# Two attention branches of a decoder's prompt stage: another order of four steps inside each beat of the pair loop

## What is computed

```
s = einsum('bqgjd,bgqnld->bgjqnl', q, k) * scale
p = masked_softmax(s, mask)
o = einsum('bgjqnl,bgqnld->bqgjd', p, v)
o = g0 * o_cmp + g1 * o_sel + g2 * o_win        # sigmoid gates
```

## Time and profile before

| what | us |
|---|---|
| median of 3 runs | 1639.38 |
| lowest, highest | 1632.87, 1643.29 |
| the profiled execution, whole time | 1641.88 |
| its span, first to last instruction | 1640.1 |
| of it the pair loop (first S to last F) | 567.9 to 806.7 |
| busy over the whole span: PE, DVE, ACT | 1461.0, 871.5, 383.5 |

### The profile page before, as it was taken

One profiled execution on the slowest core, in us unless ns is written; L12 is line 12 of the kernel. 1 busy time (PEld: TensorE's weight loads), 2 busy tenths in 40 slices (PEclk: granted clock), 3 DMA queues, 4 the chain that ended last, 5 costly groups with the idle time before them and its releaser, 6 DMA issues. The chain is left out here.

```text
span 1640.1 us, 27038 instructions
## 1 busy us (share of the span) xinstructions
PE 1461.0 (89%) x11343; PEld 1342.2 (82%) x11343; DVE 871.5 (53%) x1590; ACT 383.5 (23%) x891; POOL 82.5 (5%) x76
## 2 busy tenths in 40 slices
PE   6999899889968797989766689999989999999998
PEld 5778789789958586868543389899988999999998
DVE  3555256848633556564433355545746746465563
ACT  3543023222232344454221231000003101000000
POOL 1000001100011111111100000000000000000000
PEclk8999999999967697979678789999999999999999
DMA  9232035151321000010258442333240332323321
GB/s 351 72 116 97 13 95 184 56 201 57 119 53 53 0 1 1 2 52 2 100 190 312 175 124 79 107 99 95 91 156 26 104 104 78 103 80 99 93 88 53
DMA packets 115649, 159.03 MB, mean 97 GB/s; under 512 B 6040, under 2 KB 106840, under 8 KB 112779
## 3 DMA queue, kind: packets, MB, share of 16 engines
q1 hardware_dynamic: 111886, 122.76, 23.4%
q0 software_dynamic: 2304, 33.56, 5.1%
q10 hardware_dynamic: 1348, 1.12, 0.2%
HBM read 145.04 MB, written 16.66 MB: 99 GB/s over the span
## 5 line engine op out<-in xcount | busy, mean ns | idle before, releaser
L330 PE MATMUL ps<-uH,wh 128*128 128x260 f32 x576 | 165.9, 288 | 8.7 <-DVE wt L301 8.7
L330 PE MATMUL ps<-hH,wh 128*128 128x260 f32 x512 | 144.9, 283 | 2.6 <-DVE hT L301 2.6
L330 PE MATMUL ps<-mergedH,wh 128*128 128x260 f32 x512 | 145.7, 285 | 0.0
L330 PE MATMUL ps<-mergedT,wh 128*128 128x260 f32 x512 | 144.8, 283 | 0.0
L330 PE MATMUL ps<-hT,wh 128*128 128x260 f32 x512 | 144.8, 283 | 0.0
L330 PE MATMUL ps<-mergedH,wl 128*128 128x260 f32 x512 | 144.5, 282 | 0.0
L330 PE MATMUL ps<-hH,wl 128*128 128x260 f32 x512 | 144.5, 282 | 0.0
L457 PE MATMUL ps<-XT,w 128*128 128x256 f32 (+1 forms) x512 | 125.5, 386 | 6.3 <-DVE XT L520 6.0
L330 PEld LDWEIGHTS ps<-uH,wh 128*128 128x128 f32 x576 | 109.9, 191 | 13.6 <-DVE wt L301 8.9
L330 PE MATMUL ps<-uL,wh 128*128 128x260 f32 x384 | 109.1, 284 | 0.0
L330 PE MATMUL ps<-uH,tw 128*128 128x260 f32 x384 | 109.0, 284 | 0.0
(11 more groups left out here) (525 smaller groups left out, 3470.8 us busy)
## 6 DMA issues: line engine op xcount, KB each, us to landing
wt<-in_w_ff SPq DMA_DIRECT2D x32, 1024.0 KB, 5.4
wt<-in_w_in SPq DMA_DIRECT2D x15, 1024.0 KB, 5.7
tw<-in_w_in SPq DMA_DIRECT2D x12, 1024.0 KB, 5.3
ring<-in_cache_mem_kv SPq DMA_DIRECT2D x4, 2048.0 KB, 11.2
w<-in_cmp_w SPq DMA_DIRECT2D x8, 512.0 KB, 7.7
ring<-in_cache_win_kv SPq DMA_DIRECT2D x2, 2048.0 KB, 9.8
out_s_win<-in_cache_win_kv SPq DMA_DIRECT2D x1, 4088.0 KB
scratch_uhigh<-uH SPq DMA_DIRECT2D x1, 2080.0 KB
```

The source lines that it names most:

```text
L330: ins = pe.matmul(out, lhsT(i, c), rhs(j, c), start=(first and c == 0 and k == 0), stop=(last and c == chunks - 1 and k == 2))
```

## The change

In each beat, V(u-2) moves ahead of both turns of unit u-1 on PE. E(u) moves ahead of both copies of unit u-1 on ACT. F(u-2) moves on DVE from the end of the beat to right behind B(u) or close to it. The keys of the steps are spread anew, so the DeltaNet steps that fall in between fall in other gaps. No instruction is added or taken away, and the waits are the same.

```diff
--- before (pair_pe)
                     if u < NU:
                         scores(u)
                     yield beat(u, 0.3)
+                    if u >= 2:
+                        values(u - 2)
+                    yield beat(u, 0.55)
                     if 1 <= u <= NU:
                         turn(u - 1, 0)
-                    yield beat(u, 0.5)
-                    if u >= 2:
-                        values(u - 2)
-                    yield beat(u, 0.6)
+                    yield beat(u, 0.75)
                     if 1 <= u <= NU and rounds_of(u - 1) == 2:
                         turn(u - 1, 1)
--- before (pair_act)
                     yield beat(u, 0.35)
+                    if u < NU:
+                        exp(u)
+                    yield beat(u, 0.6)
                     if 1 <= u <= NU:
                         keep(u - 1, 0)
-                    yield beat(u, 0.55)
-                    if u < NU:
-                        exp(u)
-                    yield beat(u, 0.65)
+                    yield beat(u, 0.8)
                     if 1 <= u <= NU and rounds_of(u - 1) == 2:
                         keep(u - 1, 1)
--- before (pair_dve)
                     if u < NU:
                         biggest(u)
-                    yield beat(u, 0.8)
+                    yield beat(u, 0.45)
                     if u >= 2:
                         finish(u - 2)
                         dve.wait_ge(o_done, u - 1)
```

## The result

The changed kernel takes 1654.08 us (median of 4 runs, 1652.68 to 1659.21), the kernel before, measured beside it, 1638.47 (1632.87 to 1643.29). The ratio is 1.0093 with a 95% interval of 1.0059 to 1.0128: slower by a little under one per cent. The profiled execution of the changed kernel took 1659.21, the longest of its runs. The code ahead of the pair loop is the same, and yet the first S starts at 574.52 instead of 567.94. Over the thirteen profiled executions of this study that start lay between 564.0 and 574.5, so two spans can't be compared to better than some 10 us. The loop itself is compared more closely: from the first S to the last F it took 238.8 us before and takes 249.4 now, 10.6 more. Behind the loop the two executions differ by 0.1 us. So the 17.3 us between the two profiled executions are 6.6 ahead of the loop, which the change doesn't touch, and 10.6 in it.

The account below looks back on a forecast made before the run. PE was taken as the bound, busy 205.75 of 238.00 us in the pair loop. Terms 7.2 + 5.4 + 3.0 - 3.5 - 3.8 + 5.1 = 13.4 us on the median 1639.4 gave 1653, range 1635 to 1670.

Parts of the forecast that it names:

- beats 20 to 25: Three-tile beats 21 to 25: second turn, or E in beat 23, comes later; 7.2 us lost.
- beats 28 to 38: Four-tile beats 30 to 35: mostly later second turns, beat 32 gaining 0.5; 5.4 us lost in all.
- tail: After the last E: K(38, 0), T(38, 1), K(38, 1) and an unhidden copy join the path; 3.0 us lost.
- beats 0 to 19: One-round beats: gains from F(9), E(13) and 0.3 elsewhere; together 3.5 us gained.
- beats 26, 27: S(27) starts 0.8 us earlier and the beat after runs at full clock, 3.0; 3.8 us gained.
- clock, apart: New PE gaps bring three more low-clock stretches, each costing up to 1.75 us; 5.1 us lost.
- The second turn behind E: Two-round beats: T(u-1, 1) waits for S, B, E, K; 4.3 us after S with three tiles, 5.1 with four.
- The second rival: DeltaNet products fill the time before T(u-1, 1), leaving the tail's loss against gains: -4 us, about 1635; chance 0.17.
- F(9) and E(13): Beats 12 and 13: F(9) ahead of the second chunk's end gains 1.9 us; E(13) ahead of chunk steps, 1.3.
- The 0.8 of E(26): Beat 26: E(26) goes ahead of the third chunk's root and table load, so S(27) starts 0.8 us earlier.
- The zero for the other load: Beat 27: the table load moves to E(27), behind K(25, 1) and beside V(25), and costs nothing.
- the first rival: Two-round beats: PE's clock stays low, about 0.7 from 664 to 696; 10 us more, about 1663; chance 0.22.

Follow-up runs that it names:

- mixed kernel: The changed kernel with PE and ACT back in the old order in beats where unit u-1 has two rounds; 1636.09 us, ratio 0.9975.
- DVE-only kernel: The kernel before, with only F(u-2) moved to 0.45 of the beat on DVE, PE and ACT as before; 1638.64 us, ratio 0.9984.
- ACT-only kernel: The kernel before, with only ACT's new order, E(u) ahead of both copies of unit u-1; 1653.65 us, ratio 1.0090.
- tail_old: The changed kernel with the old order on PE and ACT for u of 39 and more; 1653.75 us, ratio 1.0091.
- beat 26, put together by hand: The kernel before, with new order in beats 0 to 14 and beat 26's PE, ACT and DVE steps reordered; 1625.76 us, ratio 0.9903.
- the mixed kernel with the early F: The mixed kernel with F(u-2) at 0.37 of the beat on DVE instead of 0.45; 1639.72 us, ratio 1.0006.

## Why the prediction was right, and where it was not

It said 1653 (1635 to 1670), and the median is 1654.08. Step by step the agreement is less even:

```
term                            predicted   measured
beats 20 to 25                      +7.2      +6.92
beats 28 to 38                      +5.4      +6.69
tail                                +3.0      +2.91
beats 0 to 19                       -3.5      -6.00
beats 26, 27                        -3.8      +0.09
clock, apart                        +5.1      in the rows above
sum                                +13.4     +10.61
```

- **The second turn behind E.** Right in place, mechanism and price. The five beats from 21 on lost 1.12, 1.91, 0.85, 1.74 and 1.34 us, for 1.35, 2.0, 0.7, 1.8 and 1.4 in the prediction. That ACT's order alone costs as much in the beats 20 to 25 (38.08), and that the mixed kernel loses all but 0.8 of it, shows the cause. What the prediction did not see is that V's new place has a price of its own there: with E back in its old place 4.7 of the 6.9 us remain, by the copy right behind the first turn. The second rival, that DeltaNet products fill the time, is refuted by the 14 waits. With four tiles the agreement of the sum, 6.69 for 5.4, hides misses. In the beats 31 and 35 I said 1.7 and 1.4, and it was 1.47 and 1.31. Beat 30 lost 2.19 for 1.7. Beat 32 gained nothing where I had 0.5, and in beat 34 I had 1.1 and it was 0.6 faster. Beat 37 I held for covered; its second turn waits 0.77 us and it costs 0.95. The five beats of the term come to 4.35; the rest is that 0.95, a loss of 2.3 by the clock in beat 28, and small gains elsewhere.
- **The tail.** 2.91 for 3.0, shown by the kernel that puts it back.
- **F(9) and E(13).** 1.81 for 1.9 and 1.40 for 1.3. F's part is shown by the DVE-only kernel, and beat 12 takes 4.9 us in all nine executions that have both new orders there. E's part is shown by the ACT-only kernel, where S(14) starts without its wait of 1.56. Its size is partly luck: with the wait gone, beat 13 took from 5.97 to 8.17 us over those nine executions, at clocks from 0.71 to 0.50, against 8.72 before.
- **Beats 26 and 27**, the step that failed: "with the gap gone, the beat after at full clock, 3.0". The 0.8 of E(26) came, with 0.67, and the gap ahead of S(27) went: S(27) starts right behind the second turn and takes 1.03 us. But two other gaps took its place, and the sum had no term for either. V(25) waits 1.65 us for F(24), which is still behind the chunk's end on DVE, and from there to the end of beat 28 PE ran mostly at half clock. And the second turn of beat 26 waits 1.44 us for a copy that stands behind the chunk's root and its table load:

```profile
707.38 0.60 ACT L1401 ACTIVATE g_sq<-ps 128x512 f32<-128x512 f32 x1 [0.52 <-PE ps L1363]
708.00 1.28 ACT L1403 ACT_TABLE_LOAD   x1
709.29 0.20 ACT L1403 ACTIVATE g_so<-g_so 128x4 f32<-128x4 f32 x1
709.40 0.46 ACT L1704 COPY XT<-ps 128x384 f32<-128x384 f32 x1
```

  The zero for the other load was right. It runs from 711.06 to 712.34, ahead of E(27), which waits for its B until 713.71; and the root above starts 0.01 us behind its load, as in the earlier trace rows. An earlier F made these beats 4.5 us shorter. The lesson is in the account: the stall that goes was priced and the one that is late next was not.
- **The clock.** "I take three" half-clock stretches more, 5.1 us. None of it came. With five gaps of 0.57 to 1.73 us in the beats 21 to 25 the clock stayed at 1.00, and so it did in the window from 756 to 800, in which the second turn of beat 34 waits longest:

```profile
770.59 0.63 PE L1631 MATMUL ps<-consts,Pb 128*128 128x128 f32 x4 [2.82 <-ACT XT L1704]
...
756.00:800.00 44.00, 39.33 (x310) 34.11 (x310) 20.91 (x44) 18.41 (x43) 5.07 (x4) 1.00 0.00 1
```

  Over the loop the mean clock rose from 0.87 to 0.90. So the first rival, a clock that stays low, did not happen, and half-clock time fell: by this share from some 62 us (0.26 of 239) to 50. That is where 2.4 us of beat 16 came from, while beat 28 lost 2.3 by it. The fall is not the change's doing for certain: `tail_old`, with the same order up to beat 38, has 0.88, so some 60 us.

That the number came out so close is in part luck. Two errors, the 5.1 of the clock and the 3.9 of the beats 26 and 27, had opposite signs. The early gain was 2.5 larger than I said in this execution, and 0.7 smaller in five others with that order. The sum for the loop, 13.4, was 2.8 above the loop's 10.6. The medians differ by 15.6, within an interval of 9.7 to 21 us, which holds both. No trace shows where the median has its other 5 us; the stages ahead of the loop scatter by 10, and the early beats of one order by 3.

## What to carry to other kernels

In a pipeline written out by hand, list for each in-order engine what a moved step now stands behind, and follow a buffer with one copy (here the bank of the turns) through that list: a step that looked free because it ran beside another becomes the longest chain of the beat once its release stands behind an operation of the same beat. Keep two orders where the units differ (one round, two rounds), and look at places where a second program's long chain ends: beat 26, put together by hand, is 2.35 us shorter at nearly the same clock, nearly as much as the whole new order is worth in the beats 0 to 19 of most executions (2.8). When a stall is removed, price the next one before its gain is booked.

## What the runs showed of the hardware that I had not expected

**The same gap does not always bring TensorE's clock down.** Three kernels have the same order in the beats 26 and 27 and the same gap ahead of S(27). Here are S(27) and a window behind it for the kernel before, the DVE-only kernel and the mixed kernel, in this order:

```profile
703.54 2.07 PE L1620 MATMUL ps<-kmT,qmT 128*128 128x256 f32 x4 [2.23 <-ACT Pb L1695]
...
703.00:713.00 10.00, 9.46 (x41) 9.00 (x42) 3.94 (x15) 2.94 (x10) 2.08 (x2) 0.50 0.00 0
```

```profile
704.87 1.92 PE L1620 MATMUL ps<-kmT,qmT 128*128 128x256 f32 x4 [2.23 <-ACT Pb L1695]
...
705.00:711.00 6.00, 6.00 (x37) 5.54 (x38) 2.15 (x9) 2.07 (x7) 1.43 (x2) 0.72 0.00 0
```

```profile
702.61 1.13 PE L1620 MATMUL ps<-kmT,qmT 128*128 128x256 f32 x4 [2.24 <-ACT Pb L1701]
...
702.00:708.00 6.00, 5.39 (x44) 5.07 (x46) 3.78 (x14) 3.12 (x10) 2.16 (x2) 1.00 0.00 0
```

Ten microseconds at 0.50, a part of six, and none: beat 27 took 9.83, 6.84 and 5.17 us. In these two beats the steps stand in the same order on PE, ACT and DVE in all three traces. So one execution may be 4.7 us off from another there by nothing in the order of these beats. In this kernel a gap of 2.23 us has a chance of costing clock and no fixed price.

**A tiny DVE operation beside GpSimd.** The multiplication of two values by two (L1776, 128x2) takes 0.16 us. Where a large GpSimd operation starts beside it, as in this timeline of the kernel before, it takes seven times that (1.12 us):

```profile
702.55 1.26 POOL L1501 TENSOR_TENSOR g_sq<-g_sq,vecs 128x512 f32<-128x512 f32 x1 [24.33 <-DVE g_sq L1477]
702.71 1.12 DVE L1776 TENSOR_TENSOR rg<-rg,gate 128x2 f32<-128x2 f32 x1
```

It belongs to F(24). In the changed kernel the same pair stands at 711.11 and 711.26, again with 1.12 us, and makes the wait of V(25) a microsecond longer; in the kernel before it also stands at the end of the second chunk, where V(10) waited. The thirteen traces together say more. They hold this operation 416 times, and 56 times it takes 0.35 to 1.13 us. Each of these 56 ends within 0.03 us of the end of a GpSimd operation on two 128x512 tensors that was running beside it, and none of the others, at 0.16 us, runs into the middle of one. So the operation is over when the GpSimd operation is, whatever was left of it. Where DVE comes to F(24) with no GpSimd operation under way, as in the mixed kernel with the early F, it takes its usual time:

```profile
703.76 0.16 DVE L1787 TENSOR_TENSOR rg<-rg,gate 128x2 f32<-128x2 f32 x1
```

Not every DVE operation waits so. The next one of F(24), L1779, reads PSUM; it starts at 703.87, a GpSimd operation of 1.26 us starts at 703.89, and it takes 0.48 us, as elsewhere.
